# Sample tokens as high and low columns: prompt groups of 512 and a packed sample tile in a feed-forward layer on one Trainium2 core

## The chip, the core and the metric

The kernel runs on one core of a Trainium2 chip. The metric is the device time in microseconds (us) of one execution. TensorE (PE) multiplies, DVE, ACT and POOL do the elementwise work, and SP issues the DMAs. Three runs of the kernel before gave 1613.31, 1614.68 and 1614.89 us.

## What is computed

One step of a decoder layer over 1024 prompt tokens and 64 sample tokens (8 sequences of 8), 1088 in all, with a model width of 1024, in float32. An input projection feeds a gated recurrence and a gated delta rule with states (the mixer); its output is projected and added to x. Then comes the part that the change is about, the feed-forward layer (width 2816), and a last norm:

```
hf = rmsnorm(x, norm2)
x = x + (jax.nn.silu(hf @ w_gate) * (hf @ w_up)) @ w_down
y = rmsnorm(x, final_norm)
```

## The kernel before

The kernel has three blocks of code that run one after the other: `input_block`, `mixer_block` and `ffn_block`. Each engine has its own program and waits on semaphores; the order of the work is the order in which the code is written. Tokens, features and weights are cut into tiles of 128.

Precision: each float32 operand is split into a high part (rounded to the type float32r, `F32R`) and a low part (the remainder, also F32R). A product is then three matmuls into the same PSUM bank, high·high, high·low and low·high; that is `mm3`, lines 84 to 88. The trace shows these three as L86, L87 and L88, wherever `mm3` is called from. Products in the mixer that are not split are plain float32 matmuls.

`ht_hi` and `ht_lo` hold the normed activations, [128 features, 8 feature tiles, 1088 tokens].

The feed-forward layer goes over 22 tiles of 128 hidden features, in 11 pairs (`pair`, first pass written out, then a hardware loop, `NP` = 11). In a pair:

- For each of its two tiles (`s`), the 1088 tokens go in three groups, `GROUPS` = 364, 364 and 360 tokens. For each group TensorE makes the gate product (`q` = 0) and the up product (`q` = 1), each 8 feature tiles × 3 matmuls, with the weights stationary and the activations streamed. Two sets of two PSUM banks (0 to 3) alternate between groups. A set is written again only when `hf` of the group before the last is done (`hf_done`).
- ACT takes the silu of the gate bank into `sg` (L1608), DVE multiplies it with the up bank into `hf` (L1654), ACT rounds this to `h_hi` (L1610), DVE makes `h_lo` (L1657).
- After the second group of the first tile, ACT and DVE split the pair's down weights into `dn_hi` and `dn_lo` (L1598, L1665); after each tile they split the gate and up weights of the next pair (`gu_hi` L1592, `gu_lo` L1635). SP loads the raw weights as soon as their buffers are free.
- The down projection goes over 9 tiles of tokens (`MT` = 9, the ninth, `NC` = 8, with the 64 sample tokens) and two halves of 512 output columns. Here `h_hi` and `h_lo` of 128 tokens (64 in the last tile) are stationary and the down weights are streamed: 2 × 3 matmuls of 512 columns for a half, in PSUM banks 4 to 7. DVE adds each half to `acc` (L1678), which started as a copy of x. TensorE waits for the add of two tiles before.

In the last pair the last norm runs along: ACT squares and sums a tile (L1628), POOL makes the root (L1691, L1693), DVE scales it into one of two buffers `y_out` (`norm_tile`, L1642), SP stores it (L1544), and the next square on the same buffer waits for that store.

The gate and up products of the very first group are issued at the end of the mixer (line 1116), where their weights are called `gu_first`; in later pairs the same buffers serve the tiles with `s` = 0.

Of the kernel before, what the change touches and what calls it, by code (L numbers as in the profile page):

```python
# [34 lines left out]
GROUPS = [(0, 364), (364, 364), (728, 360)]  # L35

# [8 lines left out]
BANK = 512  # L45
# [45 lines left out]
def build(nc, i, o, scratch):  # L91
# [7 lines left out]
    ht_hi = A("ht_hi", [P, KT, T], F32R)  # L99
    ht_lo = A("ht_lo", [P, KT, T], F32R)  # L100
# [633 lines left out]
def mixer_block(nc, i, o, scratch, psum, B, k):  # L734
# [43 lines left out]
             "samp_state ss_out0 ss_out1 ss_out2 sp_out").split()  # L778
# [63 lines left out]
    with nc.Block() as block:  # L842

        @block.sync
        def _(eng):
# [46 lines left out]
            eng.dma_start(o["S_prompt"], st[:, :, :]).then_inc(m_["sp_out"], 16)  # L892
# [21 lines left out]
            eng.wait_ge(m_["sp_out"], 16)  # L914
# [3 lines left out]
        def _(eng):  # L918
# [197 lines left out]
            m = GROUPS[0][1]  # L1116
# [347 lines left out]
def ffn_block(nc, i, o, scratch, psum, B, k):  # L1464

    ht_hi, ht_lo, normw, minus_half, eps_col = (k[n] for n in ("ht_hi", "ht_lo", "normw", "minus_half", "eps_col"))
# [5 lines left out]
    most = max(m for _, m in GROUPS)  # L1472
    sg = [B(f"sg{s}", [P, most]) for s in range(2)]
    hf = [B(f"hf{s}", [P, most]) for s in range(2)]
    fstat = B("fstat", [P, MT, 2])

# [12 lines left out]
    x1_in, n3_in = S("ff_x1_in"), S("ff_n3_in")  # L1489
# [6 lines left out]
    NG = len(GROUPS)  # L1496
    PAIR = 2 * NG
    SUMS = 2 * MT
    NP = FT // 2

    def group_of(m):

        last = min((m + 1) * P, T) - 1
        return next(n for n, (a, ln) in enumerate(GROUPS) if last < a + ln)
# [5 lines left out]
    with nc.Block() as block:  # L1510

        @block.sync
        def _(eng):
# [14 lines left out]
            eng.dma_start(normw[:, :], i["norm3"]).then_inc(n3_in, 16)  # L1528
# [12 lines left out]
            for m in range(MT):  # L1541
                n = P if m < NC else TS
                eng.wait_ge(y_done, m + 1)
                eng.dma_start(o["y"][m * P:m * P + n, :], y_out[m % 2][0:n, :]).then_inc(y_dma[m % 2], 16)  # L1544
# [4 lines left out]
        def _(eng):  # L1549
            def pair(j):  # L1550
                for s in range(2):
# [3 lines left out]
                    for g, (a, m) in enumerate(GROUPS):  # L1555
# [14 lines left out]
                for m in range(MT):  # L1570
                    n = P if m < NC else TS
                    toks = slice(m * P, m * P + n)
                    if m == 0 or group_of(m) != group_of(m - 1):
# [201 lines left out]
```

## Time and profile before

| | before |
|---|---|
| median of 3 runs | 1614.68 us |
| span of the profiled execution, first to last instruction | 1610.6 us |
| mean granted TensorE clock in it | 0.980 |
| PE, PEld (weight loads), DVE, ACT, POOL busy | 95%, 87%, 44%, 22%, 8% |
| DMA, mean over the span | 65 GB/s |

For the profiled execution the profile gives its span alone; the run times lie 2.7 to 4.3 us above it, which is what lies around the first and the last instruction. Matmul records overlap, since their ends include the way through the array: the time that a matmul takes from the next one is the step between two starts, not the length of its record. In the same way a weight load's record is longer than the step between two loads. A row that ends in [0.60 <-DVE acc L1678] says that the engine sat idle for 0.60 us before it, until that instruction was done. PEclk is the granted clock as a share of 2.4 GHz.

### The profile page before, as it was taken

Reading aid. Unit: us, or ns where it says so; the run is one execution under the profiler, and the core shown is the slowest. Engines: PE = TensorE matmul, PEld = TensorE weight load, DVE = VectorE, ACT = ScalarE, POOL = GpSimd, SP = SyncE. Lnnn points to the kernel's source line nnn. Section 1 sums busy time; section 2 is a strip of 40 time slices with the busy share of each in tenths; the row PEclk is TensorE's granted clock in tenths of the full one; section 3 lists DMA queues with packets and bytes.
Section 4 is the critical chain, followed back from the end, with each engine's and each line's share of the span. In section 5 each row is a group of like instructions: output and inputs, shape, how many; then the busy total and the mean of one; then the engine's idle time right before and its main releaser. Section 6 shows DMA issues by size and latency. Waiting matters only on the chain.

```text
span 1610.6 us, 23009 instructions
## 1 busy us (share of the span) xinstructions
PE 1533.3 (95%) x9003; PEld 1398.8 (87%) x9003; DVE 716.2 (44%) x1132; ACT 351.4 (22%) x569; POOL 132.0 (8%) x200
## 2 busy tenths in 40 slices
PE   5999999998999999998899999999999999999997
PEld 3799899997888888886598999989898989989896
DVE  5356544534566666565333333342424333332415
ACT  5354533231111111111120211112020211111012
POOL 1000000001222222211000000000000000000001
PEclk7999999997999999999899999999999999999999
DMA  5012122162122211122170201111010102010002
GB/s 195 14 43 85 53 105 91 66 209 79 40 66 65 65 59 40 64 72 72 63 277 27 75 25 57 32 46 52 26 52 26 52 26 78 26 52 26 0 0 111
DMA packets 52561, 105.12 MB, mean 65 GB/s; under 512 B 4784, under 2 KB 30320, under 8 KB 52528
## 3 DMA queue, kind: packets, MB, share of 16 engines
q1 hardware_dynamic: 52528, 104.67, 18.8%
q8 instruction: 22, 0.36, 0.1%
q14 instruction: 11, 0.09, 0.0%
HBM read 82.66 MB, written 22.00 MB: 65 GB/s over the span
## 4 chain that ended last, share of the span: by engine, by line
PE 45%; issue 2%; ACT 1%; DVE 1%; DMA 1%; POOL 0%; DVEq 0%; ACTq 0%; POOLq 0%
PE bank L86 15%; PE bank L88 15%; PE bank L87 15%; ACT gu_hi L1592 1%; DMA out_y<-y_out 1%; DVE acc L1678 0%; DVE y_out L1642 0%; DVE hf L1654 0%; ACT y_out L1628 0%; POOL fstat L1693 0%; DVEq L1677 0%; ACTq L75 0%; POOL fstat L1691 0%; POOLq L1510 0%; DVE gu_lo L1635 0%
## 5 line engine op out<-in xcount | busy, mean ns | idle before, releaser
L86 PE MATMUL bank<-ht_hi,w_hi 128*128 128x364 f32 (+1 forms) x576 | 190.4, 330 | 0.0
L88 PE MATMUL bank<-ht_hi,w_lo 128*128 128x364 f32 (+1 forms) x576 | 189.4, 329 | 0.0
L87 PE MATMUL bank<-ht_lo,w_hi 128*128 128x364 f32 (+1 forms) x576 | 189.4, 329 | 0.0
L1654 DVE TENSOR_TENSOR hf<-sg,bank 128x364 f32<-128x364 f32 (+1 forms) x66 | 35.1, 532 | 342.9 <-PE bank L88 340.8
L86 PE MATMUL bank<-ht_hi,gu_first_hi 128*128 128x364 f32 (+1 forms) x528 | 173.4, 328 | 1.4 <-PEq L842 1.4
L87 PE MATMUL bank<-ht_lo,gu_first_hi 128*128 128x364 f32 (+1 forms) x528 | 173.3, 328 | 0.0
L88 PE MATMUL bank<-ht_hi,gu_lo 128*128 128x364 f32 (+1 forms) x528 | 173.2, 328 | 0.0
L86 PE MATMUL bank<-ht_hi,gu_hi 128*128 128x364 f32 (+1 forms) x528 | 173.1, 328 | 0.0
L87 PE MATMUL bank<-ht_lo,gu_hi 128*128 128x364 f32 (+1 forms) x528 | 173.1, 328 | 0.0
L88 PE MATMUL bank<-ht_hi,gu_first_lo 128*128 128x364 f32 (+1 forms) x528 | 173.0, 328 | 0.0
L1678 DVE TENSOR_TENSOR acc<-acc,bank 128x512 f32<-128x512 f32 (+1 forms) x198 | 132.3, 685 | 90.3 <-PE bank L88 90.3
L86 PE MATMUL bank<-dn_hi,h_hi 128*128 128x512 f32 (+1 forms) x396 | 155.5, 393 | 5.9 <-DVE acc L1678 5.9
L87 PE MATMUL bank<-dn_lo,h_hi 128*128 128x512 f32 (+1 forms) x396 | 154.3, 390 | 0.0
L88 PE MATMUL bank<-dn_hi,h_lo 128*128 128x512 f32 (+1 forms) x396 | 154.2, 389 | 0.0
L1608 ACT ACTIVATE sg<-bank 128x364 f32<-128x364 f32 (+1 forms) x66 | 31.2, 473 | 370.6 <-PE bank L88 370.6
L86 PEld LDWEIGHTS bank<-ht_hi,w_hi 128*128 128x128 f32 x576 | 108.8, 189 | 0.8 <-issue 0.5
L87 PEld LDWEIGHTS bank<-ht_lo,w_hi 128*128 128x128 f32 x576 | 108.8, 189 | 0.1
L88 PEld LDWEIGHTS bank<-ht_hi,w_lo 128*128 128x128 f32 x576 | 108.8, 189 | 0.0
L86 PEld LDWEIGHTS bank<-ht_hi,gu_first_hi 128*128 128x128 f32 x528 | 99.1, 188 | 2.6 <-issue 1.5
L87 PEld LDWEIGHTS bank<-ht_lo,gu_first_hi 128*128 128x128 f32 x528 | 99.2, 188 | 0.5
L86 PEld LDWEIGHTS bank<-ht_hi,gu_hi 128*128 128x128 f32 x528 | 99.2, 188 | 0.0
L88 PEld LDWEIGHTS bank<-ht_hi,gu_lo 128*128 128x128 f32 x528 | 99.2, 188 | 0.0
(267 smaller groups left out, 2458.6 us busy)
## 6 DMA issues: line engine op xcount, KB each, us to landing
w_raw<-in_w_in SPq DMA_DIRECT2D x24, 512.0 KB, 4.2
dn_raw<-in_w_down SPq DMA_DIRECT2D x22, 512.0 KB, 4.3
scratch_qkv<-cb_y SPq DMA_DIRECT2D x12, 512.0 KB, 2.7
qkv_in<-scratch_qkv SPq DMA_DIRECT2D x8, 768.0 KB, 6.3
gu_first_raw<-in_w_gate SPq DMA_DIRECT2D x11, 512.0 KB, 3.5
gu_first_raw<-in_w_up SPq DMA_DIRECT2D x11, 512.0 KB, 4.3
gu_raw<-in_w_gate SPq DMA_DIRECT2D x11, 512.0 KB, 3.5
gu_raw<-in_w_up SPq DMA_DIRECT2D x11, 512.0 KB, 4.3
```

The costliest lines, as they stand in the source:

```text
L86: pe.matmul(out, w_hi, x_hi, start=start, stop=False)
L87: pe.matmul(out, w_hi, x_lo, start=False, stop=False)
L88: return pe.matmul(out, w_lo, x_hi, start=False, stop=stop)
L1592: eng.activation(gu_hi[s][:, :, :, :], gu_raw[s][:, :, :, :], ACT.Copy).then_inc(gu_hi_done, 1)
L1608: eng.activation(sg[b][:, 0:m], psum[2 * b][:, 0:m], ACT.Silu).then_inc(sg_done, 1)
L1654: eng.tensor_tensor(hf[b][:, 0:m], sg[b][:, 0:m], psum[2 * b + 1][:, 0:m], ALU.mult).then_inc(hf_done, 1)
L1678: eng.tensor_tensor(part, part, psum[4 + 2 * (m % 2) + half][0:n, :], ALU.add).then_inc(acc_done, 1)
```

## The change

- The feed-forward layer uses groups of its own, `FFN_GROUPS`: 512 and 512 prompt tokens, then the 64 sample tokens.
- `ht_hi` and `ht_lo` become the two halves of one tensor `ht` at the same places, so that a single access can stream the 64 high and the 64 low columns of the sample tokens as 128 columns. The sample group's products are made by `samples`: for each feature tile a matmul of the high weights with these 128 columns, and one of the low weights with the 64 high columns. The bank then holds high·high + low·high in columns 0 to 63 and high·low in 64 to 127. DVE copies the second half out into `xlo` and adds the two, for gate and for up.
- `h_hi` of the sample tokens is followed by their low part, as 128 stationary columns. In the down projection the sample tile ("packed") needs four matmuls for a half: two of these 128 columns with `dn_hi` (128 rows out) and two of the 64 high ones with `dn_lo` (64 rows out). The rows 64 to 127 of the ninth tile of `acc` start as zeros (memset) and collect the low part; in the last pair DVE copies them to rows 0 to 63 of a free buffer and adds them ("fold").
- The tiles of the down projection come in the order `TILES`: 0 to 5, the sample tile, 6, 7. The last norm and the stores follow this order.
- `sp_out` and `n3_in` are merged into other semaphores.

```diff
+FFN_GROUPS = [(0, BANK), (BANK, BANK), (SEQ, TS)]
...
-    ht_hi = A("ht_hi", [P, KT, T], F32R)
-    ht_lo = A("ht_lo", [P, KT, T], F32R)
+    ht = A("ht", [P, 2, KT, T], F32R)
+    ht_hi, ht_lo = ht[:, 0], ht[:, 1]
...
-            m = GROUPS[0][1]
+            m = FFN_GROUPS[0][1]
...
-    h_hi = B("h_hi", [P, 2, T], F32R)
-    h_lo = B("h_lo", [P, 2, T], F32R)
+    h_hi = B("h_hi", [P, 2, T + TS], F32R)
+    h_lo = B("h_lo", [P, 2, SEQ], F32R)
...
+    TILES = [0, 1, 2, 3, 4, 5, NC, 6, 7]
+    FOLD = TILES.index(NC)
...
         @block.tensor
         def _(eng):
+            def samples(out, w, f):
+
+                both = lambda: eng.matmul(out[:, 0:2 * TS], w[0], ht[:, :, f, SEQ:T], start=f == 0, stop=f == KT - 1)
+                low = lambda: eng.matmul(out[:, 0:TS], w[1], ht_hi[:, f, SEQ:T], start=False, stop=False)
+                if f < KT - 1:
+                    both()
+                    return low()
+                low()
+                return both()
...
-                                mm = mm3(eng, psum[b + q][:, 0:m], gu_hi[s][:, q, f, :], gu_lo[s][:, q, f, :],
-                                         ht_hi[:, f, a:a + m], ht_lo[:, f, a:a + m], f == 0, f == KT - 1)
+                                w = (gu_hi[s][:, q, f, :], gu_lo[s][:, q, f, :])
+                                if a == SEQ:
+                                    mm = samples(psum[b + q], w, f)
+                                else:
+                                    mm = mm3(eng, psum[b + q][:, 0:m], *w,
+                                             ht_hi[:, f, a:a + m], ht_lo[:, f, a:a + m], f == 0, f == KT - 1)
...
+                        if m < NC:
+                            for s in range(2):
+                                mm = mm3(eng, out[:, :], h_hi[:, s, toks], h_lo[:, s, toks],
+                                         dn_hi[:, s, cols], dn_lo[:, s, cols], s == 0, s == 1)
+                        else:
+                            eng.matmul(out[:, :], h_hi[:, 0, toks], dn_hi[:, 0, cols], start=True, stop=False)
+                            for s in range(2):
+                                eng.matmul(out[0:TS, :], h_hi[:, s, SEQ:T], dn_lo[:, s, cols], start=False, stop=False)
+                            mm = eng.matmul(out[:, :], h_hi[:, 1, toks], dn_hi[:, 1, cols], start=False, stop=True)
...
         @block.scalar
...
+                        gate = psum[2 * b][:, 0:m]
+                        if a == SEQ:
+                            gate = hf[b][:, TS:2 * TS]
+                            eng.wait_ge(x_part, 4 * (2 * j + s) + 2)
...
         @block.vector
...
+                        up = psum[2 * b + 1][:, 0:m]
+                        if a == SEQ:
+                            eng.wait_ge(gu_mm, 2 * n + 1)
+                            eng.tensor_copy(xlo[:, 0, :], psum[2 * b][:, TS:2 * TS]).then_inc(x_part, 1)
+                            eng.wait_ge(x_part, 4 * (2 * j + s) + 1)
+                            eng.wait_ge(h_lo_done, n - 1)
+                            eng.tensor_tensor(hf[b][:, TS:2 * TS], psum[2 * b][:, 0:TS], xlo[:, 0, :],
+                                              ALU.add).then_inc(x_part, 1)
+                            eng.wait_ge(gu_mm, 2 * n + 2)
+                            eng.tensor_copy(xlo[:, 1, :], psum[2 * b + 1][:, TS:2 * TS]).then_inc(x_part, 1)
+                            eng.wait_ge(x_part, 4 * (2 * j + s) + 3)
+                            eng.tensor_tensor(xlo[:, 1, :], psum[2 * b + 1][:, 0:TS], xlo[:, 1, :],
+                                              ALU.add).then_inc(x_part, 1)
...
+                    if not more and p == FOLD:
+                        low = gu_raw[1][0:TS, 0].rearrange("p f n -> p (f n)")
+                        eng.wait_ge(acc_done, SUMS * j + 2 * p + 2)
+                        eng.tensor_copy(low, acc[TS:2 * TS, NC, :]).then_inc(folded, 1)
+                        eng.wait_ge(folded, 2)
+                        eng.tensor_tensor(acc[0:TS, NC, :], acc[0:TS, NC, :], low, ALU.add).then_inc(folded, 1)
...
+            eng.memset(acc[TS:P, NC, :], 0.0).then_inc(folded, 1)
```

On TensorE, in the first pair, the last matmuls of the second group and the first of the third were, before the change (`gu_first_hi` and `gu_first_lo` are the weights of the first tile, "128x360" is the shape of the output):

```order
L88 MATMUL bank<-ht_hi,gu_first_lo 128x364
L86 MATMUL bank<-ht_hi,gu_first_hi 128x360
L87 MATMUL bank<-ht_lo,gu_first_hi 128x360
L88 MATMUL bank<-ht_hi,gu_first_lo 128x360
```

and are now, where `mm3` stands at lines 87 to 89 and `samples` at 1561 and 1562:

```order
L89 MATMUL bank<-ht,gu_first_lo 128x512
L1561 MATMUL bank<-ht,gu_first_hi 128x128
L1562 MATMUL bank<-ht,gu_first_lo 128x64
L1561 MATMUL bank<-ht,gu_first_hi 128x128
L1562 MATMUL bank<-ht,gu_first_lo 128x64
```

So the third group has 32 matmuls instead of 48, half of them with 128 columns and half with 64.

On TensorE, in the down projection, the two halves of the sample tile were the last of a pair:

```order
L88 MATMUL bank<-dn_hi,h_lo 128x512
L86 MATMUL bank<-dn_hi,h_hi 64x512
L87 MATMUL bank<-dn_lo,h_hi 64x512
L88 MATMUL bank<-dn_hi,h_lo 64x512
```

and now stand between the tiles 5 and 6:

```order
L89 MATMUL bank<-dn_hi,h_lo 128x512
L1607 MATMUL bank<-dn_hi,h_hi 128x512
L1609 MATMUL bank<-dn_lo,h_hi 64x512 x2
L1610 MATMUL bank<-dn_hi,h_hi 128x512
L1607 MATMUL bank<-dn_hi,h_hi 128x512
```

A half has four matmuls of 512 columns instead of six. On DVE, the sample group of the first tile has now these steps, with what each waits for:

```order
L1689 COPY xlo<-bank 128x64 [waits gu_mm]
L1692 TENSOR_TENSOR hf_4407<-bank,xlo 128x64 [waits h_lo_done,x_part]
L1695 COPY xlo<-bank 128x64 [waits gu_mm]
L1697 TENSOR_TENSOR xlo<-bank,xlo 128x64 [waits x_part]
L1705 TENSOR_TENSOR hf_4407<-sg_4405,xlo 128x64 [waits sg_done,h_lo_done,gu_mm,x_part]
```

The first four are new, ahead of the product into `hf`.

## Rows read from the trace of the kernel before

**Rows 1.** The page, part 1: busy us, share of the span, instructions.
```profile
PE 1533.3 (95%) x9003; PEld 1398.8 (87%) x9003; DVE 716.2 (44%) x1132; ACT 351.4 (22%) x569; POOL 132.0 (8%) x200
```

**Rows 2.** Timeline of PE (start us, us, instruction): a pair's two tiles, and what follows.
```profile
1234.58 0.33 PE L86 MATMUL bank<-ht_hi,gu_first_hi 128*128 128x364 f32 x1
...
1258.48 0.33 PE L86 MATMUL bank<-ht_hi,gu_hi 128*128 128x364 f32 x1
...
1282.34 0.40 PE L86 MATMUL bank<-dn_hi,h_hi 128*128 128x512 f32 x1
```

**Rows 3.** Timeline of DVE in a down projection: adds after each half.
```profile
1145.22 0.69 DVE L1678 TENSOR_TENSOR acc<-acc,bank 128x512 f32<-128x512 f32 x1 [0.67 <-PE bank L88]
...
1158.82 0.69 DVE L1678 TENSOR_TENSOR acc<-acc,bank 128x512 f32<-128x512 f32 x1 [0.67 <-PE bank L88]
1160.20 0.68 DVE L1678 TENSOR_TENSOR acc<-acc,bank 64x512 f32<-64x512 f32 x1 [0.69 <-PE bank L88]
```

**Rows 4.** Stretches: length, busy us (PE, PEld, DVE, ACT, POOL), PEclk, DMA share, GB/s.
```profile
499.30:500.90 1.60, 1.60 (x18) 1.60 (x16) 0.85 (x2) 1.12 (x2) 0.00 (x0) 1.00 0.00 0
742.30:749.10 6.80, 4.59 (x20) 3.93 (x21) 2.67 (x3) 2.16 (x10) 2.37 (x3) 0.60 0.28 87
1234.58:1282.34 47.76, 47.76 (x289) 47.76 (x288) 10.68 (x14) 9.09 (x14) 0.00 (x0) 1.00 0.13 44
...
744.51 1.97 PE L946 MATMUL bank<-cst,xn 128*128 128x128 f32 x8 [3.31 <-DVE xn L1251]
```

**Rows 5.** Timeline of weight loads (PEld) and of PE, float32 products in the mixer.
```profile
499.17 1.86 PEld L970 LDWEIGHTS bank<-cst,xn 128*128 128x128 f32 x16
500.96 0.30 PEld L975 LDWEIGHTS bank<-kg,cst 128*128 128x128 f32 x2
...
719.58 1.01 PEld L970 LDWEIGHTS bank<-cst,xn 128*64 128x64 f32 x16 [0.20 <-issue]
720.61 0.19 PEld L975 LDWEIGHTS bank<-kg,cs 64*64 64x64 f32 x2
...
482.14 0.61 PE L1028 MATMUL bank<-inv_t,pp 128*128 128x128 f32 x4
...
483.48 0.61 PE L1033 MATMUL bank<-pp,inv_t 128*128 128x128 f32 x4
```

**Rows 6.** Groups of weight loads by form: busy us, mean ns.
```profile
L86 PEld LDWEIGHTS bank<-ht_hi,gu_hi 128*128 128x128 f32 x528 | 99.2, 188 | 0.0
L1063 PEld LDWEIGHTS bank<-state,q_in 128*128 128x128 f32 x64 | 7.8, 192 | 0.0
L86 PEld LDWEIGHTS bank<-dn_hi,h_hi 128*64 128x64 f32 x44 | 5.9, 134 | 3.6
L970 PEld LDWEIGHTS bank<-cst,xn 128*64 128x64 f32 x16 | 1.0, 138 | 0.2 <-issue 0.2
```

**Rows 7.** Timelines of PE and ACT where mixer and feed-forward meet.
```profile
801.49 0.71 PE L946 MATMUL bank<-cst,xn 64*128 64x64 f32 x8
803.44 1.28 ACT L1608 ACT_TABLE_LOAD   x1 [0.80 <-PEq L842]
```

**Rows 8.** Timelines of ACT and DVE in the last pair, and the stores.
```profile
1578.77 1.06 ACT L1628 ACTIVATE y_out<-acc 128x1024 f32<-128x1024 f32 x1 [2.39 <-DVE acc L1678]
...
1593.70 1.28 DVE L1642 SCALAR_TENSOR_TENSOR y_out<-acc,fstat,normw 128x1024 f32<-128x1024 f32 x1 [0.96 <-POOL fstat L1693]
1596.42 1.28 DVE L1642 SCALAR_TENSOR_TENSOR y_out<-acc,fstat,normw 128x1024 f32<-128x1024 f32 x1 [0.24 <-POOL fstat L1693]
1599.86 1.28 DVE L1642 SCALAR_TENSOR_TENSOR y_out<-acc,fstat,normw 128x1024 f32<-128x1024 f32 x1 [0.96 <-POOL fstat L1693]
...
out_y<-y_out SPq DMA_DIRECT2D x8, 512.0 KB, 2.6
```

**Rows 9.** Timelines of DVE and PE where a down projection starts.
```profile
1282.70 0.53 DVE L1654 TENSOR_TENSOR hf<-sg,bank 128x360 f32<-128x360 f32 x1 [6.29 <-PE bank L88]
...
1288.55 0.50 PE L86 MATMUL bank<-dn_hi,h_hi 128*128 128x512 f32 x1 [0.60 <-DVE acc L1678]
```

More of the change, by code:

```diff
@@ L44 @@
 SAMPLE_LEVELS = 3
-BANK = 512
 class Plan:
@@ L1499, in ffn_block, with rows_of @@
     NP = FT // 2
+    TILES = [0, 1, 2, 3, 4, 5, NC, 6, 7]
+    FOLD = TILES.index(NC)
+    folded, x_part = S("folded"), S("x_part")
+    def rows_of(m):
+        return P if m < NC else TS
     def group_of(m):
         last = min((m + 1) * P, T) - 1
-        return next(n for n, (a, ln) in enumerate(GROUPS) if last < a + ln)
+        return next(n for n, (a, ln) in enumerate(FFN_GROUPS) if last < a + ln)
     def first(n):
@@ L1540, in _ @@
             loop(eng, NP - 1, pair)
[L1541 to L1544, printed above, removed]
+            for p, m in enumerate(TILES):
+                n = rows_of(m)
+                eng.wait_ge(y_done, p + 1)
+                eng.dma_start(o["y"][m * P:m * P + n, :], y_out[p % 2][0:n, :]).then_inc(y_dma[p % 2], 16)
             eng.wait_ge(y_dma[0], 16 * (MT // 2 + 1))
@@ L1554, in pair @@
                     eng.wait_ge(gu_lo_done, 2 * j + s)
-                    for g, (a, m) in enumerate(GROUPS):
+                    for g, (a, m) in enumerate(FFN_GROUPS):
                         n = PAIR * j + NG * s + g
@@ L1569, in pair @@
                 eng.wait_ge(dn_lo_done, 2 * j + 2)
[L1570 to L1573, printed above, removed]
+                for p, m in enumerate(TILES):
+                    toks = slice(m * P, (m + 1) * P)
+                    if p == 0 or group_of(m) > max(group_of(q) for q in TILES[:p]):
                         eng.wait_ge(h_lo_done, PAIR * j + NG + group_of(m) + 1)
@@ L1669, in pair @@
                 if isinstance(j, int) and j == 0:
-                    eng.wait_ge(x1_in, 32)
-                for m in range(MT):
-                    n = P if m < NC else TS
-                    if not more and m >= 2:
-                        norm_tile(m - 2)
-                    for half in range(2):
-                        part = acc[0:n, m, half * BANK:(half + 1) * BANK]
-                        eng.wait_ge(dn_mm, SUMS * j + 2 * m + half + 1)
-                        eng.tensor_tensor(part, part, psum[4 + 2 * (m % 2) + half][0:n, :],
-                                          ALU.add).then_inc(acc_done, 1)
+                    eng.wait_ge(x1_in, 48)
+                    eng.wait_ge(folded, 1)
+                for p, m in enumerate(TILES):
+                    if not more and p >= 2:
+                        norm_tile(p - 2)
+                    for half in range(2):
+                        part = acc[:, m, half * BANK:(half + 1) * BANK]
+                        eng.wait_ge(dn_mm, SUMS * j + 2 * p + half + 1)
+                        eng.tensor_tensor(part, part, psum[4 + 2 * (p % 2) + half][:, :], ALU.add).then_inc(acc_done, 1)
+                    if not more and p == FOLD:
[5 more added lines that the diff above has]
+            eng.memset(acc[TS:P, NC, :], 0.0).then_inc(folded, 1)
             loop(eng, NP - 1, lambda j: pair(j, True))
```

73 lines of the change are left out of this document (39 added, 34 removed).

## The prediction, made before the changed kernel ran

> **What bounds the kernel now.** I read the page's busy shares first [rows 1]: TensorE is busy for 95% of the span; DVE (44%) and ACT (22%) have room. "Busy" hides how fast it works, since its matmuls overlap in the records, so the next view is the timeline of starts. In one pair of feed-forward tiles the gate and up products run without a gap from 1234.58 to 1258.48 us and from there to 1282.34 us [rows 2]: 144 matmuls in 23.90 and 23.86 us, **166 ns each for 360 to 364 columns**. In the down projection DVE's adds follow the halves: ten halves of six 512-column matmuls take 1158.82 − 1145.22 = 13.60 us, **226.7 ns a matmul**; a half of the 64-token tile takes 1.38 us, 230 ns a matmul [rows 3]. Column time at 2.4 GHz (the granted clock is 1.00 there [rows 4]) is 151.7 ns for 364 columns and 213.3 ns for 512; 14 and 13 ns are left over. So at these sizes a matmul costs its columns plus some 14 ns, and the weight loads are hidden.
>
> **What the change makes of the columns.** Before, each weight slice of a tile (22 tiles × gate and up × 8 slices = 352) gets 9 matmuls with 3 × 1088 = 3264 columns. After, it gets six of 512, one of 128 and one of 64: again 3264. Nothing is saved but one start; it is the price of the two short matmuls that decides.
>
> **What a short matmul costs.** No row shows this kernel's split type (float32r) with fewer than 360 columns, so I bound it from both sides. Low end: columns plus 14 ns, 67 and 41 ns. High end: the load of the weights. Float32 products show it; there the trace has two records for each matmul of the code, each with its own weight load. Line 970 streams a single column: its 16 loads of 128 weight columns run from 499.17 to 500.96 us, **112 ns each**, and with 64 weight columns from 719.58 to 720.61 us, 64 ns each [rows 5]. So with next to nothing to stream, the load sets the pace. With 128 streamed columns (lines 1028, 1033) the step is again 111 ns (12 records from 482.14 to 483.48 us). Is a float32r load as slow? Its record is 188 ns with 128 weight columns and 134 with 64; the float32 load's is 192 and 138 [rows 6]. Same length, same 0.84 ns per weight column. Both short matmuls here load 128 weight columns. I take **112 ns for each**, because the load rows match so closely.
>
> Then a sample group is 32 × 0.112 = 3.58 us and a tile 96 × 0.2267 + 3.58 = 25.34 us instead of 23.88: +1.46 us, **22 × 1.46 = +32.1 us**. Its first 48 matmuls at full width are in the mixer, 48 × 61 ns = 2.9 us of that sum; they are on the path, as line 946's transposes follow at once at 801.49 us, and the feed-forward block starts when those are read out [rows 7].
>
> The Trainium skill has a smaller price: "TensorE: Matmul & The Clock Gate", section "Back-to-back issue gap", gives about 81 ns for a sustained load-and-matmul at 128 columns (bf16). By it a sample group would take 2.59 us and the total would come to about 1617 us. Rows 5 show 111 to 112 ns for 4-byte operands, so I side with the rows. The same page, Part 3, "The mechanism", says that a weight load overlaps running matmuls only when its row group differs. By it load and stream would add up, which is rival 4; the step of 166 ns in rows 2, barely above the columns alone, disagrees.
>
> **Packed tile in the down projection.** A half of the sample tile had six matmuls, 1.38 us. Now it has two with 128 weight columns and two with 64, 2 × 0.2267 + 2 × 0.230 = 0.91 us: −0.47 us, twice a pair. DVE's add of 0.69 us still fits into that. In ten pairs this is on the path, **−9.3 us**. In the eleventh TensorE does not set the end.
>
> **The tail.** From the first square on, the last pair goes by the two output buffers: square, the two POOL steps, DVE's scale, a store of 2.6 us, then the next square on this buffer, 6.16 us for two tiles [rows 8]. The fold puts a copy and an add of 1024 columns into DVE after the seventh tile's adds, some 1.2 us each (the scale of 1024 columns takes 1.28). DVE is then free 2.4 us later than now; following the chain, the scale now at 1596.42 comes 2.2 us late, the one at 1599.86 comes 1.3 us late, and the last tile hangs on the latter: +1.3 us. That last tile has 128 rows, not 64: up to +0.3 us. **+1.6 us.**
>
> **Costed at nothing.** The four small DVE steps per sample group (about 0.2 us each, as 360 columns take 0.53 and 512 take 0.69 us [rows 3, 9]) lie in DVE's idle time; in the first half of a pair they queue behind dn_lo, done by my estimate 5 us after the prompt groups, and TensorE first needs them before the group after next, 14 us after. At the end of a pair they replace a step of 0.53 us ahead of the chain to gu_hi, gu_lo and the first add, behind which TensorE idles some 0.9 us [rows 9]; that chain stays as long to within 0.1 us (±1 us in all), and if it grew, each us would cost ten. The memset of 1 us runs while ACT loads its table [rows 7]. The merged semaphores wait for loads that landed long before.
>
> Sum: +32.1 − 9.3 + 1.6 = +24.4 us on a span of 1610.6, so 1635.0. The runs' median is 4.1 us above that span, so I forecast **1639.1 us**.
>
> **Rivals.** (1) *Float32r weights load at twice the speed* and a short matmul takes the 64 ns of the 64-column rows. The sample group is 2.06 us, the tile 23.82, together −1.3 − 9.3 + 1.6 = −9.0 us: **1605.7 us, faster**. It decides below 77 ns a short matmul, where the tile's loss is under the 7.7 us gained elsewhere. For it: no row shows float32r loads at their limit. Against: the load records in rows 6. Chance 10%. (2) *Halfway* between the 64 and the 112 ns rows, 88 ns: a load partly hidden. 2.82 us a group, +15.5 − 7.7, 1622.5 us. Nothing in the rows asks for it. Chance 7%, of which 2% for paces from 72 to 82 ns, within 3.2 us of no change. (The 81 ns of the skill's page would lie there.) (3) *Columns alone count*, 67 and 41 ns: 1.73 us a group, −8.6 − 7.7, 1598 us, 2%; rows 5 speak against it. (4) *The load is not hidden*: 112 ns comes on top of 53 and 27 ns, 4.86 us a group, 28 us more than forecast, 1667 us. Rows 2 speak against it. 2%. (That is what the Part 3 rule of the skill's page would give.) (5) *The clock drops.* The sample group streams for a third of its time only. At 742.30 to 749.10 us the granted clock was 0.60 on average, after TensorE had sat idle for 3.3 us [rows 4]; such a stretch loses 0.4 × 6.8 = 2.7 us, and after each of 22 sample groups it would cost 60 us: 1699 us. The single-column burst kept 1.00 [rows 4], but lasts only 1.8 us. 3%.
>
> **The numbers.** The forecast case has 76%; its own range is 1632 to 1647 us (a pace of 107 to 115 ns gives −4 to +2 us, the pair's chain ±1, the tail −1 to +2, the runs' distance from the span ±1). To leave no more than 2 in 10 out the range reaches down through the halfway case: 1618 to 1648 us. A measurement of this kernel can tell 0.2%, 3.2 us. Faster: rivals 1 and 3, 12%. Within 0.2%: the lower part of rival 2, 2%. Slower: 76 + 5 + 2 + 3 = 86%.
>
> **What would show it.** In the profile after: the samples' matmuls 112 ns apart (32 in 3.6 us), with TensorE's weight loads back to back there; a tile's gate and up products 25.3 us; a packed half 0.91 us; an unchanged wait for line 1678's add once a pair; the granted clock 1.00 all through the pairs; a tail from the first square some 1.5 us longer than the 1610.6 − 1578.8 = 31.8 us of now [rows 8]. Sample matmuls at 64 ns or less would make the sign wrong; at 85 ns, only the size.

## The result, and the profile after

The changed kernel took 1655.87 us (median of four runs, 1654.12 to 1660.97), the kernel before, run beside it, 1613.99 us. The ratio is **1.027**, 95% interval 1.025 to 1.029: slower, and by 42 us, not by 24. Its profiled execution has a span of 1654.5 us against 1610.6, +43.9 us, at the same mean granted clock (0.979 and 0.980).

The page's first part of the kernel after, to be held against [rows 1]:

```profile
PE 1576.6 (95%) x8607; PEld 1350.6 (82%) x8607; DVE 736.1 (44%) x1223; ACT 352.1 (21%) x569; POOL 132.4 (8%) x200
```

Nearly 400 matmuls fewer, and yet TensorE is busy for longer; the share of 95% is the same. What differs is the time per matmul, so the timeline of PE is the view to read. Here is one pair of the changed kernel, as [rows 2] had it of before: first prompt matmul, first sample matmul (L1561), then the same for the second tile, and the start of the down projection.

```profile
1178.99 0.39 PE L87 MATMUL bank<-ht,gu_first_hi 128*128 128x512 f32 x1
...
1201.48 0.22 PE L1561 MATMUL bank<-ht,gu_first_hi 128*128 128x128 f32 x1
...
1205.00 0.45 PE L87 MATMUL bank<-ht,gu_hi 128*128 128x512 f32 x1
...
1227.53 0.22 PE L1561 MATMUL bank<-ht,gu_hi 128*128 128x128 f32 x1
```

The sample group takes 1205.00 − 1201.48 = 3.52 us, **110 ns a matmul**; 112 was forecast. The 96 prompt matmuls take 1201.48 − 1178.99 = 22.49 us, **234 ns each**; forecast was 226.7. A tile is then 26.01 us (26.05 for the second), not 25.34. In every one of the 22 tiles it is so, but for those that the clock disturbs.

In the down projection the adds of DVE show both step times that were forecast, 1.36 us for a half of a prompt tile and 0.92 us for a half of the packed one [rows 3]:

```profile
1247.86 0.69 DVE L1729 TENSOR_TENSOR acc<-acc,bank 128x512 f32<-128x512 f32 x1 [0.67 <-PE bank L89]
1249.22 0.69 DVE L1729 TENSOR_TENSOR acc<-acc,bank 128x512 f32<-128x512 f32 x1 [0.67 <-PE bank L89]
1250.14 0.69 DVE L1729 TENSOR_TENSOR acc<-acc,bank 128x512 f32<-128x512 f32 x1 [0.23 <-PE bank L1610]
1251.06 0.69 DVE L1729 TENSOR_TENSOR acc<-acc,bank 128x512 f32<-128x512 f32 x1 [0.23 <-PE bank L1610]
1252.42 0.69 DVE L1729 TENSOR_TENSOR acc<-acc,bank 128x512 f32<-128x512 f32 x1 [0.67 <-PE bank L89]
```

So the same 512-column matmul costs 227 ns here (six in 1.36 us) and 234 ns in gate/up.

The third difference is the granted clock. Timeline of PE around a sample group's end, and stretches of the same pair (length, busy us of PE, PEld, DVE, ACT, POOL, then PEclk, DMA share, GB/s):

```profile
1282.16 0.31 PE L1561 MATMUL bank<-ht,gu_first_hi 128*128 128x128 f32 x1
1282.31 0.57 PE L87 MATMUL bank<-ht,gu_hi 128*128 128x512 f32 x1
1282.67 0.63 PE L88 MATMUL bank<-ht,gu_hi 128*128 128x512 f32 x1
1283.10 0.63 PE L89 MATMUL bank<-ht,gu_lo 128*128 128x512 f32 x1
...
1285.66 0.50 PE L89 MATMUL bank<-ht,gu_lo 128*128 128x512 f32 x1
1286.00 0.39 PE L87 MATMUL bank<-ht,gu_hi 128*128 128x512 f32 x1
```
```profile
1256.30:1278.79 22.49, 22.49 (x98) 18.11 (x97) 2.07 (x3) 1.83 (x3) 0.00 (x0) 1.00 0.00 0
1278.79:1282.31 3.52, 3.52 (x34) 3.52 (x32) 2.22 (x3) 2.44 (x3) 0.00 (x0) 1.00 0.00 0
1282.31:1285.80 3.49, 3.49 (x11) 2.75 (x11) 2.70 (x8) 1.06 (x4) 0.00 (x0) 0.52 0.18 27
```

Right behind this sample group the clock is at 1.2 GHz for 3.4 us: the step is 0.43 us instead of 0.23. Five of the 22 sample groups are followed by such a stretch, each costing 0.7 to 1.7 us; the kernel before has none in its pairs. The sample group itself ran at full clock and without a gap. (The Trainium skill, "TensorE: Matmul & The Clock Gate", section "HAM oscillation — how this bites in real kernels", blames such falls on gaps in which TensorE idles. Here TensorE was busy for 3.52 of 3.52 us.)

**Where 43.9 us come from**, by the starts in the two timelines. Tiles: 22 × (26.03 − 23.88) = +47.3. Down projection, 24.48 us instead of 25.42 in ten pairs: −9.4. Stretches of low clock from the first tile to the last tile's end: +4.7. From the start of the last down projection to the end: 37.6 instead of 35.5 us, +2.1, of which 1.7 are the fifth stretch of low clock (its first nine matmuls 427 ns apart). Gate/up starts 0.8 us earlier, at 792.58 instead of 793.39. Sum +43.9.

### The profile page after: what moved, and what is told of

It reads as the page before. It is cut to its first block, busy times and chain, and to the rows that moved or that the text cites. A ratio compares the mean times of both kernels' runs of the same rounds, so it can differ in the third digit from the quotient of the medians.

```text
span 1654.5 us, 22415 instructions
## 1 busy us (share of the span) xinstructions
PE 1576.6 (95%) x8607; PEld 1350.6 (82%) x8607; DVE 736.1 (44%) x1223; ACT 352.1 (21%) x569; POOL 132.4 (8%) x200
## 4 chain that ended last, share of the span: by engine, by line
PE 47%; DVE 1%; issue 1%; ACT 1%; DMA 0%; POOL 0%; DVEq 0%; POOLq 0%; ACTq 0%
PE bank L87 14%; PE bank L88 14%; PE bank L89 13%; PE bank L1561 3%; PE bank L1562 2%; ACT gu_hi L1621 1%; PE bank L1609 1%; DVE acc L1729 1%; DMA out_y<-y_out 0%; DVE y_out L1678 0%; PE bank L1610 0%; PE bank L1607 0%; ACT y_out L1664 0%; DVE hf L1705 0%; DVE xlo L1695 0%
## 5 line engine op out<-in xcount | busy, mean ns | idle before, releaser
L87 PE MATMUL bank<-ht,w_hi 128*128 128x364 f32 (+1 forms) x576 | 190.0, 330 | 1.0 <-DVE w_lo L544 1.0
L89 PE MATMUL bank<-ht,w_lo 128*128 128x364 f32 (+1 forms) x576 | 189.1, 328 | 0.0
L88 PE MATMUL bank<-ht,w_hi 128*128 128x364 f32 (+1 forms) x576 | 188.9, 328 | 0.0
L87 PE MATMUL bank<-dn_hi,h_hi 128*128 128x512 f32 x352 | 140.7, 400 | 4.0 <-DVE acc L1729 4.0
L87 PE MATMUL bank<-ht,gu_hi 128*128 128x512 f32 x352 | 141.6, 402 | 0.0
L87 PE MATMUL bank<-ht,gu_first_hi 128*128 128x512 f32 x352 | 139.8, 397 | 1.4 <-PEq L843 1.4
L88 PE MATMUL bank<-ht,gu_hi 128*128 128x512 f32 x352 | 141.0, 401 | 0.0
L89 PE MATMUL bank<-ht,gu_lo 128*128 128x512 f32 x352 | 140.6, 400 | 0.0
L89 PE MATMUL bank<-ht,gu_first_lo 128*128 128x512 f32 x352 | 139.7, 397 | 0.0
L88 PE MATMUL bank<-ht,gu_first_hi 128*128 128x512 f32 x352 | 139.6, 397 | 0.0
L88 PE MATMUL bank<-dn_lo,h_hi 128*128 128x512 f32 x352 | 139.2, 395 | 0.0
L89 PE MATMUL bank<-dn_hi,h_lo 128*128 128x512 f32 x352 | 138.9, 395 | 0.0
L87 PEld LDWEIGHTS bank<-ht,w_hi 128*128 128x128 f32 x576 | 108.4, 188 | 2.1 <-issue 1.9
L88 PEld LDWEIGHTS bank<-ht,w_hi 128*128 128x128 f32 x576 | 108.4, 188 | 0.1
```

Of the source, the lines that this page charges most:

```text
L87: pe.matmul(out, w_hi, x_hi, start=start, stop=False)
L88: pe.matmul(out, w_hi, x_lo, start=False, stop=False)
L89: return pe.matmul(out, w_lo, x_hi, start=False, stop=stop)
```

## The experiments

Single matmuls below are read from starts in the timeline of one pair, as above. Cycles are those of 2.4 GHz.

### The parts of the change

**packed_364**: the change without its groups; the prompt and sample tokens stay together as 364, 364 and 360. Since the last group then holds prompt and sample tokens, DVE makes its low part in two steps instead of one (not shown below).

```diff
-FFN_GROUPS = [(0, BANK), (BANK, BANK), (SEQ, TS)]
+FFN_GROUPS = GROUPS
```

> The packed sample tile of the down projection alone; the gate and up products keep their groups of 364, 364 and 360 tokens. If the short matmuls of the sample group are what costs, this gives 9.3 us in ten pairs and loses about 0.5 us in the tail (the fold, as measured in the changed kernel): about 8 to 9 us less than before, 1605 to 1606 us, and the granted clock stays 1.00 in the pairs. If the packed tile itself or the waits around it were to blame, it is no faster than before.

1603.41 us against 1613.27, ratio 0.9937 (0.992 to 0.9954): 9.9 us less, where 8 to 9 were expected. The only low clock in the gate and up products is in the first tile. The packed tile is a gain of 10 us by itself, and all of the loss lies in what this run leaves out, the new groups.

**no_samples**: of the 32 sample matmuls of a tile two are left (those of the last feature tile); the samples' gate and up products are not made.

> The changed kernel with 2 instead of 32 matmuls in a sample group (the last slice's only, so the samples' feed-forward output is left wrong). Theory load: a tile loses 30 x 0.110 = 3.3 us, 73 us in all, and since no stretch with a low streaming share is left, no clock drop either: 75 to 82 us less than the changed kernel, 1574 to 1581 us. The prompt groups keep their 233 ns a matmul. Rival (the sample groups slow the prompt groups down around them): the prompt matmuls come back to 227 ns and it is 14 us faster still.

1622.38 us: only 34 us less than the changed kernel, where 75 to 82 were expected. Timelines of PE at a tile's end and at a pair's boundary:

```profile
1187.66 0.33 PE L1563 MATMUL bank<-ht,gu_first_hi 128*128 128x128 f32 x2
1188.76 0.50 PE L87 MATMUL bank<-ht,gu_hi 128*128 128x512 f32 x1 [0.76 <-DVE hf L1708]
...
1216.84 0.39 PE L89 MATMUL bank<-dn_hi,h_lo 128*128 128x512 f32 x1
1220.07 0.50 PE L87 MATMUL bank<-dn_hi,h_hi 128*128 128x512 f32 x1 [2.84 <-DVE acc L1732]
```

Without the 3.5 us of sample matmuls TensorE runs into DVE: it idles 0.8 us between the tiles (eleven times, 8.2 us in all), and up to 2.9 us for the add that is queued behind the splits of the next weights. Ten such waits sum to 28.4 us, and behind seven of them the clock is low for 3.4 us. The expectation had put these waits at nothing. The prompt step is still 234 ns. So the sample group is also cover for DVE, and the 234 ns are not its doing.

**half_weights**: the sample matmuls load 64 instead of 128 weight columns, so half of the samples' hidden features are not made.

```diff
-both = lambda: eng.matmul(out[:, 0:2 * TS], w[0], ht[:, :, f, SEQ:T], ...)
-low = lambda: eng.matmul(out[:, 0:TS], w[1], ht_hi[:, f, SEQ:T], ...)
+both = lambda: eng.matmul(out[0:64, 0:2 * TS], w[0][:, 0:64], ht[:, :, f, SEQ:T], ...)
+low = lambda: eng.matmul(out[0:64, 0:TS], w[1][:, 0:64], ht_hi[:, f, SEQ:T], ...)
```

> The changed kernel with only 64 of the 128 stationary weight columns in the sample group's matmuls (rows 64 to 127 of these products are left out, so the output is wrong). Theory load (a float32r weight column takes 0.83 ns to load): the short matmuls go from 110 ns to about 64 ns, or to the 67 ns of 128 streamed columns for every other one; a group takes 2.0 to 2.1 us instead of 3.52, about 32 us less in all, and with a higher streaming share fewer clock drops. Theory of a fixed start cost: 110 ns stays.

1625.34 us, 30.5 us less than the changed kernel; about 32 were expected. The group, with as many matmuls and streamed columns as before, takes 1.89 us instead of 3.52:

```profile
1191.52 0.22 PE L1561 MATMUL bank<-ht,gu_first_hi 128*64 128x128 f32 x1
...
1193.41 0.45 PE L87 MATMUL bank<-ht,gu_hi 128*128 128x512 f32 x1
```

59 ns a matmul against 110: **the weight columns are the price of a short matmul**, as the prediction had it from [rows 5]. And behind none of the 22 groups is the clock low.

**three_64**: 46 short matmuls in a sample group instead of 32; the high weights' one matmul of 128 columns becomes two of 64, but for the first feature tile, which keeps the one, and the last, which keeps it and gets one of 64 besides.

```diff
+hi = lambda n: eng.matmul(out[:, n * TS:(n + 1) * TS], w[0], ht[:, n, f, SEQ:T], start=False, stop=False)
+if f == 0:
+    both()
+    return low()
+hi(0)
 if f < KT - 1:
-    both()
+    hi(1)
     return low()
```

> The changed kernel with 46 instead of 32 matmuls in a sample group: high times high and high times low as two matmuls of 64 columns except at the ends (the last slice's high times high is counted twice, so the samples' output is wrong). Theory load: every short matmul costs 110 ns whatever its columns, so a tile takes 14 x 0.110 = 1.54 us more, +34 us, and the clock drops more often than 5 times. Theory columns: the same columns in more pieces cost next to nothing more.

1738.17 us, +82 instead of +34. Timeline of PE in one group, and the group as a stretch:

```profile
1157.14 0.42 PE L1561 MATMUL bank<-ht,gu_first_hi 128*128 128x128 f32 x2
1157.40 0.24 PE L1562 MATMUL bank<-ht,gu_first_lo 128*128 128x64 f32 x1
...
1159.37 0.40 PE L1562 MATMUL bank<-ht,gu_first_lo 128*128 128x64 f32 x1
1159.58 0.61 PE L1563 MATMUL bank<-ht,gu_first_hi 128*128 128x64 f32 x2
1160.01 0.40 PE L1562 MATMUL bank<-ht,gu_first_lo 128*128 128x64 f32 x1
```
```profile
1154.77:1160.90 6.13, 6.13 (x48) 6.13 (x46) 4.10 (x6) 2.78 (x4) 0.00 (x0) 0.82 0.00 0
```

At full clock the step is about that of the 32 matmuls (1154.77 to 1157.14: 21 in 2.37 us, 113 ns), so the 14 more would cost the +34 us expected. From 1159.37 on two matmuls take 0.43 us: the clock has fallen within the group, though PE and PEld are busy for 6.13 of 6.13 us. It stays low for 6.8 us, at nineteen of the 22 groups. That is rival 5 in earnest: with 46 short matmuls on end the clock comes down in nearly every group, however busy the record says TensorE is.

### Why a prompt matmul takes 234 ns

**zeros**: the normed input of the feed-forward layer is all zeros, and so are all its products.

```diff
-eng.scalar_tensor_tensor(out=xn[0:t.n, :], in0=x_in[0:t.n, :], scalar=stat[0:t.n, 1:2],
-                         in1=normw[0:t.n, :], op0=ALU.mult, op1=ALU.mult).then_inc(m_["xn_done"], 1)
+eng.tensor_tensor(xn[0:t.n, :], x_in[0:t.n, :], x_in[0:t.n, :], ALU.subtract).then_inc(m_["xn_done"], 1)
```

> The changed kernel with zeros as the input of the feed-forward layer (the second norm is replaced by x minus x), so gate, up, hidden values and the down products are all zero. If the 233 ns of the prompt matmuls against 227 ns in the down projection depends on the values, both change, towards the 213 ns of the columns alone. If it depends on where the streamed operand lies or how it is read, 233 and 227 ns stay. The clock drops after sample groups stay if they depend on activity in time alone.

1655.01 us, steps unchanged (234, 227, 110 ns), and the low clock came behind three sample groups. Values play no part in the steps, and the clock falls without them too.

**groups_512_288**: the kernel before with groups of 512, 288 and 288 tokens and no other edit.

> The kernel before with feed-forward groups of 512, 288 and 288 tokens: as many matmuls and columns as before. Theory per column (a column from ht costs 1.095 clock periods of 2.4 GHz, and nothing is paid per matmul): 233 ns and 131 ns, a tile of 23.8 us as before, the same time as before. Theory per matmul (columns at 2.4 GHz plus 14 ns): 227 and 134 ns, which gives the same total; the two steps tell them apart.

1616.6 us. Timeline of PE: 48 matmuls of 512 columns, then 96 of 288.

```profile
1164.21 0.39 PE L86 MATMUL bank<-ht_hi,gu_first_hi 128*128 128x512 f32 x1
...
1175.45 0.29 PE L86 MATMUL bank<-ht_hi,gu_first_hi 128*128 128x288 f32 x1
...
1188.25 0.40 PE L86 MATMUL bank<-ht_hi,gu_hi 128*128 128x512 f32 x1
```

234.2 ns (562 cycles, 50 more than the columns) and 133.3 ns (320 cycles, 32 more). [Rows 2] gave 36 more for 364. So the slow step is not made by the sample groups nor by `ht` as one tensor; it comes up in the kernel before as soon as its groups have 512 columns.

**down_streams_ht**: the down projection streams columns of ht instead of the down weights, so its sums are others. **shift_32**: the kernel before with all buffers 32 bytes further on. **two_rows**: gate/up's prompt groups stream feature tiles 0 and 1 only, so their products are others. **banks_swapped**: gate/up in PSUM banks 4 to 7, down in 0 to 3.

```diff
-                                         dn_hi[:, s, cols], dn_lo[:, s, cols], s == 0, s == 1)
+                                         ht_hi[:, s, cols], ht_lo[:, s, cols], s == 0, s == 1)
```
```diff
     normw = A("normw", [P, D])
+    A("pad", [P, 8])
```
```diff
-ht_hi[:, f, a:a + m], ht_lo[:, f, a:a + m], f == 0, f == KT - 1)
+ht_hi[:, f % 2, a:a + m], ht_lo[:, f % 2, a:a + m], f == 0, f == KT - 1)
```
```diff
-mm = mm3(eng, psum[b + q][:, 0:m], *w,
+mm = mm3(eng, psum[4 + b + q][:, 0:m], *w,
```

> The changed kernel, but the down products stream ht_hi and ht_lo (their first two feature tiles) instead of dn_hi and dn_lo, except in the packed tile; y is wrong. The prompt matmuls of gate and up take 233 ns for 512 columns, those of down 227 ns, and values play no part. If the extra 6 ns belong to the streamed tensor (where ht lies), the down matmuls go to 233 ns: 192 per pair more than now by 6.7 ns, 11 pairs, minus the packed ones, about +6 us. If they belong to the stationary side or to the bank written, they stay at 227 ns.

> The kernel before with a pad of 32 bytes ahead of ht, so that ht, the weights and all that follows move from addresses that are 32 past a multiple of 64 to multiples of 64 (ht itself to a multiple of 256). If the alignment of the streamed rows causes the time above the columns' own (14 ns at 364, 13 ns at 512 columns), it falls, by up to 9% of TensorE's time. If not, the time is as before within 0.2%.

> The changed kernel with only the feature tiles 0 and 1 of ht streamed in the prompt groups (outputs wrong); those are the rows that the down projection streamed at 227 ns in the run down_streams_ht. If the step depends on which rows of ht are streamed, it goes from 233 to 227 ns; if on the stationary operand or the bank, it stays.

> The changed kernel with the PSUM banks of the two products exchanged in the feed-forward layer: gate and up in banks 4 to 7, down in 0 to 3. If the step goes with the bank, gate and up take 227 ns and down 233 ns; otherwise nothing changes, 1655 us.

None of the four changed a step. down_streams_ht: 227 ns in the down projection, 1655.36 us. shift_32: ratio 0.9995 (0.9984 to 1.0007), and each of its six groups of a pair takes the same time as before to 0.01 us. two_rows: 234.3 ns, 1655.95 us. banks_swapped: 234.2 ns, 1653.76 us. So it is not the streamed tensor, not the rows of it that follow each other, and not the bank. A common shift of everything by 32 bytes does nothing either; that was tried at 360 and 364 columns in gate and up, and at 512 in the down projection.

**stationary_ht**: in the prompt groups the stationary operand is 128 columns of ht instead of the weights, so the prompt products of gate and up are others.

```diff
-mm = mm3(eng, psum[b + q][:, 0:m], *w,
+mm = mm3(eng, psum[b + q][:, 0:m], ht_hi[:, f, 0:P], ht_lo[:, f, 0:P],
```

> The changed kernel with 128 columns of ht_hi and ht_lo in place of the gate and up weights as stationary operand of the prompt groups (all prompt outputs are wrong). Streamed rows and bank stay. If the step of 233 ns for 512 columns, against 227 ns in the down projection, comes with the weights as stationary operand, it goes to 227 ns (14 us less in all). If it comes with the streamed rows or the bank, it stays at 233 ns.

1641.08 us, and the step is short:

```profile
1175.95 0.39 PE L87 MATMUL bank<-ht 128*128 128x512 f32 x1
...
1197.71 0.22 PE L1561 MATMUL bank<-ht,gu_first_hi 128*128 128x128 f32 x1
```

96 in 21.76 us, **226.7 ns**. The extra goes with the stationary operand: with where it lies, or with how it is made. By the kernel's own layout (`Plan`) ht, h_hi and dn_hi begin at the same place within 256 bytes in each partition, and so do mix_hi and wo_hi, whose product ends the mixer. In down the step is 227 ns; of that last product twelve matmuls take 792.58 − 789.82 = 2.76 us, 230 ns each, as the 64-row ones of [rows 3]. In gate/up of the changed kernel ht begins 160 bytes further on, within 256, than the weights. Shifting everything, as shift_32 did, leaves these distances alone. So three kernels move the weights of gate and up (and, behind them, the raw buffer `dn_raw0`, which no matmul reads):

```diff
-    B = Plan(nc, gu_at)
+    B = Plan(nc, gu_at + 160)
     gu_first_hi, gu_first_lo = (B(f"gu_first_{n}", [P, 2, KT, P], F32R) for n in ("hi", "lo"))
...
+    B.at += 160
     gu_hi = [first_hi, B("gu_hi1", [P, 2, KT, P], F32R)]
```

> The changed kernel with the four buffers of gate/up weights (the stationary operand of the gate and up products) 32 bytes further on in SBUF, nothing else. Theory A (the position of the stationary columns against the streamed ones within 64 bytes sets the extra of a matmul; now ht lies at 32 bytes past a multiple of 64 and the weights at 0, in every product with the short step the two agree): the 512-column step in gate/up goes from 234 to 227 ns, tile 25.3 instead of 26.0 us, kernel about 1641 to 1643 us. Rival B (something else of these weights, for instance which engine writes them or that a DMA fills their neighbours): the step stays at 234 ns and the kernel at 1654 to 1656 us.

> Control: the same with 64 bytes, which moves the weights but leaves their position within 64 bytes as it was. Theory A: the step stays at 234 ns, time 1652 to 1656 us. If any move of the buffers were to make the step short, it would be 227 ns here too.

> The same with 160 bytes instead of 32, so that the weights and ht agree within 256 bytes and not only within 64. If the unit that counts is 64 bytes (or 128), the step is 227 ns here and in the kernel with 32 bytes; if it is 256 bytes, it is 227 ns here and 234 ns there; if position plays no part, 234 ns in both.

The timeline of PE in gu_plus160 (its L1562 is L1561 of the changed kernel), where weights and ht begin at the same place within 256 bytes:

```profile
1172.59 0.39 PE L87 MATMUL bank<-ht,gu_first_hi 128*128 128x512 f32 x1
...
1194.35 0.22 PE L1562 MATMUL bank<-ht,gu_first_hi 128*128 128x128 f32 x1
```

And in gu_plus32:

```profile
1183.34 0.40 PE L87 MATMUL bank<-ht,gu_first_hi 128*128 128x512 f32 x1
...
1205.65 0.22 PE L1562 MATMUL bank<-ht,gu_first_hi 128*128 128x128 f32 x1
```

| distance of weights and ht within 256 bytes | kernel | 96 prompt matmuls | step, 512 columns | time |
|---|---|---|---|---|
| 160 | the changed kernel | 22.49 us | 234.3 ns | 1655.87 us |
| 128 | gu_plus32 | 22.31 us | 232.4 ns | 1655.0 us (1651.84 to 1666.40) |
| 96 | gu_plus64 | 22.40 us | 233.3 ns | 1649.02 us (one run) |
| 0 | gu_plus160 | 21.76 us | 226.7 ns | 1636.78 us (one run) |

Theory A as I had put it, 64 bytes, fell: 32 bytes did not make the step short. A distance of 0 within 256 bytes did, in both slots of weights. Since only the weights moved, this alone would also fit their own place instead of their distance from ht. Against that speaks the kernel before, whose second slot of weights lies 96 bytes off the first within 256. Here is the first group of each tile from [rows 2], 48 matmuls of the same 364 streamed columns:

```profile
1242.58 0.33 PE L86 MATMUL bank<-ht_hi,gu_first_hi 128*128 128x364 f32 x1
...
1266.41 0.33 PE L86 MATMUL bank<-ht_hi,gu_hi 128*128 128x364 f32 x1
```

1242.58 − 1234.58 = 8.00 us with the first slot (distance 160) and 1266.41 − 1258.48 = 7.93 us with the second (distance 64), 36 and 32 cycles over the columns. shift_32 moves both slots by 32 bytes, and ht with them, and gives 8.00 and 7.93 us again: other places, the same distances, the same steps. At 512 columns distance and place were not separated in this way.

gu_plus160, timed once more:

> The kernel of gu_plus160 once more, timed against the kernel before. If its single time (1636.8 us) was typical, the median is 1636 to 1640 us, 15 to 19 us under the changed kernel, of which 22 tiles x 96 x 7.5 ns = 15.8 us are the step; above that only in runs in which the clock falls in the sample groups. If the single time was luck, the median is over 1645 us.

1635.24 us (1635.01 to 1638.77), ratio to the kernel before 1.0138 (1.012 to 1.0156). That is 20.6 us under the changed kernel's median for a padding of 160 bytes, or 18.6 us when each is held against the kernel before that ran beside it. Of it 22 × 96 × 7.6 ns = 16.1 us are the step; the rest fits less time at the low clock (two stretches behind sample groups in the profiled execution, none in that of gu_plus160, five in the changed kernel). It is near the 1639.1 us that the prediction had from its 226.7 ns.

### A version that beats both

**late_split** is packed_364 with one of DVE's steps moved: the low part of the next pair's second gate and up weights is made after the adds of the first two down tiles, not before them.

```diff
-                    if more:
+                    if more and s == 0:
                         split_gu(j + 1, s)
...
                         eng.tensor_tensor(part, part, psum[4 + 2 * (p % 2) + half][:, :], ALU.add).then_inc(acc_done, 1)
+                    if more and p == 1:
+                        split_gu(j + 1, 1)
```

> packed_364 with one more edit: at the end of a pair DVE makes the low part of the next pair's second gate and up weights (2.29 us) after the adds of the first two down tiles instead of ahead of them. TensorE's wait for the first add, 0.9 us in ten pairs, should go: about 8 us less than packed_364, near 1595 us. If another wait takes its place (the adds after the split come late), part of that is lost and shows as a wait for a later add.

1595.82 us, ratio 0.9895 (0.9879 to 0.9912), 7.6 us under packed_364. TensorE's wait for the add [rows 9] is gone: timeline of PE, the down projection from its first matmul to the next pair's.

```profile
1201.15 0.40 PE L87 MATMUL bank<-dn_hi,h_hi 128*128 128x512 f32 x1
...
1224.75 0.33 PE L87 MATMUL bank<-ht,gu_first_hi 128*128 128x364 f32 x1
```

23.60 us against 25.42 before: 104 matmuls of 226.9 ns and nothing else. **late_groups** moves the first slot of weights to distance 0 (the second stays at 64) and changes the group sizes, and **all_groups** takes the same groups into the input stage (the first two edits are in both, the last in all_groups alone):

```diff
-FFN_GROUPS = [(0, BANK), (BANK, BANK), (SEQ, TS)]
+FFN_GROUPS = [(0, 384), (384, 352), (736, 352)]
...
-    B = Plan(nc, gu_at)
+    B = Plan(nc, gu_at + 160)
...
-GROUPS = [(0, 364), (364, 364), (728, 360)]
+GROUPS = [(0, 384), (384, 352), (736, 352)]
```

> The kernel with the packed tile alone and DVE's late split (three prompt groups, 1595.8 us), with two edits on top: the weights lie so that they agree with ht within 64 bytes in both slots, and the groups are 384, 352 and 352 columns instead of 364, 364 and 360, so that every group begins at a multiple of 64 bytes. Theory A: a step costs its columns plus 32 cycles at 2.4 GHz, 173.3 and 160.0 ns, a tile 23.68 us instead of 23.88 to 23.90, over 22 tiles 4 to 5 us less: 1591 to 1592 us. Rival B: the extra stays at about a tenth of the columns, the tile at 23.9 us and the kernel at 1595 to 1596 us.

> late_groups with the input stage's prompt groups also 384, 352 and 352 columns (its weights lie 64 bytes from ht within 256, as those of one slot of the feed-forward layer do, where these groups run at their columns plus 32 cycles). Theory: an input tile falls from 11.92 us to 24 x (173.3 + 2 x 160.0) ns = 11.84 us; over some 30 tiles 2 to 3 us less than late_groups: 1590 to 1591.5 us. Rival: the evacuations or the convolution, whose pieces change size, are late somewhere, and the time is that of late_groups or above.

late_groups: 1593.21 us, ratio 0.9875 (0.9859 to 0.9892). Its tiles take 23.68 us to the hundredth, columns plus 32 cycles:

```profile
1153.15 0.33 PE L87 MATMUL bank<-ht,gu_first_hi 128*128 128x384 f32 x1
...
1176.83 0.33 PE L87 MATMUL bank<-ht,gu_hi 128*128 128x384 f32 x1
...
1185.15 0.32 PE L87 MATMUL bank<-ht,gu_hi 128*128 128x352 f32 x1
...
1200.51 0.40 PE L87 MATMUL bank<-dn_hi,h_hi 128*128 128x512 f32 x1
```

22 × 0.2 us = 4.4 us less; 1.5 us of it were lost in the profiled execution to a low clock in the first tile (27.50 instead of 26.06 us). The medians differ by 2.6 us, and the ranges of the two kernels' times overlap, so the steps show this gain and the times alone do not. The gain is not the finding above. The second slot's weights lie where they lay in late_split, 64 bytes off ht, and there only the sizes changed. Its tile in late_split:

```profile
1177.29 0.33 PE L87 MATMUL bank<-ht,gu_hi 128*128 128x364 f32 x1
```

From there to the down projection at 1201.15 us it takes 23.86 us, and in late_groups 1200.51 − 1176.83 = 23.68. So in this slot the group sizes alone brought it. In the first slot, 23.90 to 23.69 us, both were changed.

all_groups: **1588.96 us** (1588.3 to 1590.06), ratio 0.9852 (0.9834 to 0.987), 23 us under the kernel before and some 65 under the changed one. It is 4.3 us under late_groups, where 2 to 3 were expected; in its input stage sizes alone changed, and a tile there (72 matmuls) takes 11.84 us instead of 11.92.

## Why the prediction was wrong

The sign and the chain of reasons held; the size did not, and the time fell above the range (1655.87, over 1648). The span grew by 43.9 us instead of 24.4. The miss of 19.5 us is, to 0.1 us, the tiles +15.2, the clock +6.4, the tail without its clock −1.1, the packed tile −0.1 and an earlier start −0.8. By its steps:

- **The price of a short matmul**: right. 110 ns measured, 112 forecast, 1.3 us too much over the kernel. half_weights shows the cause, 59 ns with 64 weight columns. Rivals 1 to 4 fell with it. (The Trainium skill's 81 ns, "TensorE: Matmul & The Clock Gate", section "Back-to-back issue gap", was too low for these operands. The rule of its Part 3, "The mechanism", that a weight load overlaps running matmuls only when its row group differs, did not hold here: load and stream would then add up as in rival 4, to 152 ns on average, and 110 were measured.)
- **"a tile 96 × 0.2267"**: this term failed. 226.7 ns was read from the down projection's adds and carried over to gate/up, where both operands are others. There it is 234.3 ns: 22 × 96 × 7.6 ns = 16 us, most of the miss of 19.5 us. What the runs showed in its place is that the step depends on the two operands and not on the columns alone: with the gate and up weights moved to distance 0 from ht it is the 226.7 ns of the sum (gu_plus160). The warning was in the rows: [rows 2] gave 36 cycles over the columns in gate/up where [rows 3] gave 32 in down. I rounded both to "some 14 ns". A difference of less than 2 ns at 364 columns was nearly eight at 512.
- **Rival 5, the clock**: I gave it 3% and priced it as all or nothing. It came behind five of 22 groups, 1.7 us where it fell whole: 6.4 us in the profiled execution. The changed kernel's runs lie 6.9 us apart, and the slowest has the lowest mean granted clock (0.977, the fastest 0.982), which fits more such stretches. That the single-column burst kept its clock [rows 4] told nothing of a group twice as long.
- **Packed tile**: right, −9.4 us against −9.3, and packed_364 alone −9.9.
- **Tail**: +1.6 forecast; +2.1 measured, but that the two are near is luck. 1.7 of it are the clock, and the fold and the larger last tile cost only about 0.5 (in packed_364, without low clock there, 35.9 instead of 35.5 us from the last down projection on). The fold was put too dear: copy and add are 1.9 us, not 2.4; where the rest of the 1.1 us went was not traced. Timeline of DVE:

```profile
1639.52 0.70 DVE L1733 COPY gu_raw<-acc 64x1024 f32<-64x1024 f32 x1
1640.26 1.22 DVE L1735 TENSOR_TENSOR acc<-acc,gu_raw 64x1024 f32<-64x1024 f32 x1
```

- **Costed at nothing**: right here. The boundary wait did not grow. Here it is by the views of PE's waits (total us, times, longest) of the kernel before, of the changed kernel, and of no_samples, which shows how thin the cover is:

```profile
PE bank L86 <- DVE acc L1678: 5.9, 10, 0.6
```
```profile
PE bank L87 <- DVE acc L1729: 4.0, 8, 0.5
```
```profile
PE bank L87 <- DVE acc L1732: 28.4, 10, 2.9
```

What stays open: why the position costs what it does, and at which sizes. At 512 columns the runs show the distance 0 within 256 bytes as fast and 96, 128 and 160 as slow; 32, 64, 192 and 224 were not tried. A group that starts further on in ht has another distance than the first one, so smaller sizes were run at more of them. Tiles of 384, 352 and 352 columns come to 32 cycles over the columns on average, with distances of 0 and 128 in one slot and 64 and 192 in the other, and 288 columns come to 32 at distances of 160 and 32. Groups of 364 and 360 columns come to 35 to 37 in five cases of six, a distance of 0 (360 columns, first slot) among them. So distance is not the whole rule, and in these runs the size of the group decides with it. Why the clock fell behind five groups and not behind seventeen like ones was not settled either.

## What to carry to other kernels

Take the step time of a matmul from a row with the same operands, not only with the same shape, and look at its excess over the columns in cycles, before rounding: two products that differed by four cycles at 364 columns differed by eighteen at 512. A matmul that streams less than its weights take to load costs the load, so count weight columns, not streamed ones, when columns are split into thin groups; and look at the granted clock behind a long run of them, though TensorE is never idle. Before DVE or ACT work is called free, ask what covers it, and whether the change takes that cover away. And where a run changes two things, look for a part of the kernel in which only one of them changed: here the second slot of weights told what the whole time could not.

## What the runs showed of the hardware that I had not expected

- The step of a float32r matmul of 512 columns depends on where the weights lie: 544 cycles if weights and ht begin at the same place within 256 bytes, and 558 to 562 at distances of 96 to 160 bytes. A padding of 160 bytes was worth 16 us by the steps and 19 to 21 by the times, of 1656. With groups of 288, 352 or 384 columns no such extra showed.
- The granted clock fell to 1.2 GHz while TensorE's record was busy throughout: behind groups of 32 short matmuls (3.5 us) in five of 22 cases, in or behind groups of 46 in nearly all, and behind none of the groups of 32 that took 1.9 us.
- The load of 128 weight columns is what a short matmul costs in float32r as in float32 (110 and 112 ns); 64 columns cost 59 ns.
